# First mixer attention: two heads' scores issued alternately, value outputs in the transposes' banks

## What is computed

```python
def chunked_relpos_attention(h, w_in, q_gain, k_gain, rel_bias, w_out):
    q, k, v = jnp.split(h @ w_in, 3, axis=-1)
    q = rms_norm(q.reshape(B, S, A_HEADS, A_HEAD_DIM), q_gain) * (A_HEAD_DIM ** -0.5)
    k = rms_norm(k.reshape(B, S, A_HEADS, A_HEAD_DIM), k_gain)
    ...
        s = jnp.einsum('bihd,bjhd->bhij', qc, kb).astype(jnp.float32) + bias
        s = jnp.where(valid[None, None, None, :], s, -jnp.inf)
        p = jax.nn.softmax(s, axis=-1).astype(vb.dtype)
        return jnp.einsum('bhij,bjhd->bihd', p, vb)
    ...
    return o @ w_out
```

## Time and profile before

| what | value |
|---|---|
| median of 3 runs | 1064.32 us (1062.67 to 1066.03) |
| the profiled execution | 1061.2 us |
| its span in the trace | 1059.5 us |
| PE, DVE, ACT, POOL busy | 1027.4, 766.1, 550.7, 100.5 us |
| mean granted clock of PE | 0.99 |
| the 19 turns on PE | about 80 to 167 us of the span |

### The profile page before, as it was taken

The page is one execution under the profiler, slowest core; times in us unless marked ns, Lnnn a source line. Parts: engine busy times, 40 slices in busy tenths (PEclk is TensorE's granted clock), DMA queues, the critical chain, the costliest instruction groups (busy, mean ns, idle before and its releaser), DMA issues.

```text
span 1059.5 us, 17084 instructions
## 1 busy us (share of the span) xinstructions
PE 1027.4 (97%) x6050; PEld 898.3 (85%) x6050; DVE 766.1 (72%) x1368; ACT 550.7 (52%) x918; POOL 100.5 (9%) x160
## 2 busy tenths in 40 slices
PE   6999999999999999999999999999999999999997
PEld 5888788899999988889999899999988887778875
DVE  5688878987888677787778756555568786586863
ACT  1457666634545456744444445444346676566662
POOL 0031201000000010010010000000003021030210
PEclk9999999999999989999999999999999999999999
DMA  9876656688787648867685455665436640175401
GB/s 366 297 264 219 228 210 219 202 321 294 266 277 269 232 154 292 294 199 262 207 277 203 140 189 161 197 212 193 161 109 225 201 157 21 66 262 185 165 9 41
DMA packets 57198, 218.46 MB, mean 206 GB/s; under 512 B 6421, under 2 KB 11541, under 8 KB 51001
## 3 DMA queue, kind: packets, MB, share of 16 engines
q1 hardware_dynamic: 48368, 169.24, 46.6%
q0 software_dynamic: 6048, 43.52, 11.6%
q10 hardware_dynamic: 2728, 5.00, 1.5%
HBM read 216.67 MB, written 1.06 MB: 205 GB/s over the span
## 4 chain that ended last, share of the span: by engine, by line
PE 90%; DVE 5%; DMA 2%; ACT 2%; issue 1%; POOL 0%; SPq 0%; ACTq 0%; DVEq 0%
PE ps L1743 26%; PE ps L1744 25%; PE ps L1745 25%; PE ps L1847 2%; PE ps L2225 2%; PE ps L1802 1%; PE ps L1812 1%; DVE w_lo L1008 1%; PE ps L2273 1%; PE ps L2115 1%; PE ps L1792 1%; PE ps L1997 1%; DMA arena<-in_adastream 1%; DMA raw<-in_wstream 1%; PE ps L2254 1%
## 5 line engine op out<-in xcount | busy, mean ns | idle before, releaser
L1008 DVE TENSOR_TENSOR w_lo<-raw,w_hi 128x1024 fp32r<-128x1024 f32 (+1 forms) x312 | 356.2, 1182 | 61.7 <-ACT w_hi L554 56.6
L554 ACT ACTIVATE w_hi<-raw 128x1024 fp32r<-128x1024 f32 (+1 forms) x312 | 307.1, 1021 | 133.7 <-DMA raw<-in_wstream 95.6
L1743 PE MATMUL ps<-h_hi,w_hi 128*128 128x256 f32 x704 | 200.9, 285 | 0.3
L1745 PE MATMUL ps<-h_hi,w_lo 128*128 128x256 f32 x704 | 199.2, 283 | 0.0
L1744 PE MATMUL ps<-h_lo,w_hi 128*128 128x256 f32 x704 | 199.2, 283 | 0.0
L1743 PE MATMUL ps<-w_hi,h_hi 128*128 128x512 f32 (+1 forms) x480 | 191.6, 399 | 7.7 <-DVE h_lo L1087 3.0
L1744 PE MATMUL ps<-w_lo,h_hi 128*128 128x512 f32 (+1 forms) x480 | 185.4, 386 | 0.0
L1745 PE MATMUL ps<-w_hi,h_lo 128*128 128x512 f32 (+1 forms) x480 | 185.3, 386 | 0.0
L1743 PE MATMUL ps<-w_hi,a_hi 128*128 128x512 f32 x352 | 137.3, 390 | 0.7 <-DVE a_lo L1461 0.7
L1743 PEld LDWEIGHTS ps<-h_hi,w_hi 128*128 128x128 f32 x704 | 135.0, 192 | 3.4 <-DVE h_lo L1087 1.3
L1744 PE MATMUL ps<-w_lo,a_hi 128*128 128x512 f32 x352 | 137.2, 390 | 0.0
(11 more groups left out here) (221 smaller groups left out, 1330.6 us busy)
## 6 DMA issues: line engine op xcount, KB each, us to landing
raw<-in_wstream SPq DMA_DIRECT2D x296, 512.0 KB, 5.2
ada_raw<-in_adastream POOLq DMA_DIRECT2D x40, 1024.0 KB, 5.2
ada_raw<-in_adastream SPq DMA_DIRECT2D x4, 1024.0 KB, 9.2
arena<-in_adastream SPq DMA_DIRECT2D x4, 1024.0 KB, 10.8
row<-in_gate_rows ACTq DMA_DIRECT2D x5, 512.0 KB, 4.9
raw<-in_wsmall SPq DMA_DIRECT2D x16, 128.0 KB, 2.2
row<-in_params POOLq DMA_DIRECT2D x2, 769.0 KB, 5.5
x<-in_x SPq DMA_DIRECT2D x1, 1024.0 KB, 9.2
```

The source lines that it names most:

```text
L554: act.activation(w_hi[:, c % SPLIT, at], raw[:, n, 0:width // 2], ACT.Copy)\
L1008: nc.vector.tensor_tensor(w_lo[:, c % SPLIT, at], raw[:, (2 * c + h) % RAW, 0:width // 2], w_hi[:, c % SPLIT, at].bitcast(F32), ALU.subtract)\
L1743: nc.tensor.matmul(dst, sh, mh, start=start, stop=False)
L1745: return nc.tensor.matmul(dst, sl, mh, start=False, stop=stop)
```

## The change

Scores are issued in even turns only, for heads h and h + 1 together: `score_pair(h)` alternates between head h in partitions 0 to 63, into bank 4, and head h + 1 in partitions 64 to 127, into bank 5. Value products go to columns 384 to 511 of bank 6 or 7, beside the transposes, and these now wait for the normalisation (`s_norm`) instead of ACT's copy. Units 2, 3, 6 and 7 go through banks 2, 3, 0 and 1, which are banks of the projection; the waits of turns 6 to 8 change with that. Output groups go to banks 2, 5, 5 and 4. The first group's steps move later: on PE to the end of turn 9, on ACT and DVE from turn 7 to turn 9.

```diff
-HEAD_BANK = (4, 5, 4, 5, 4, 5, 5, 5, 5, 4, 5, 4, 4, 5, 4, 5, 5, 4, 5)
-UNIT_BANK = {0: 4, 1: 5, 4: 6, 5: 7, 2: 4, 3: 4, 6: 5, 7: 4}
+UNIT_BANK = {0: 4, 1: 5, 4: 6, 5: 7, 2: 2, 3: 3, 6: 0, 7: 1}
-OUT_BANK = (4, 5, 4, 4)
+OUT_BANK = (2, 5, 5, 4)
...
@@ ACT, turn h
                 if h == 7:
                     hankel(act, 12, gate[:]).then_inc(s_late[1], 16)
                     hi_part(13, 1, CW)
-                    out_hi(0)
...
                 if h in (8, 9):
                     hi_part(15, h - 8, CW)
+                if h == 9:
+                    out_hi(0)
...
@@ DVE, turn h
                     lo_part(13, 1, CW)
-                    out_lo(0)
...
                 if h in (9, 10):
                     lo_part(15, h - 9, CW)
+                if h == 9:
+                    out_lo(0)
...
@@ PE
-            def bank_read(h):
...
+            def score_pair(h):
+
+                pe.wait_ge(s_qklo, (3, 4, 7, 8)[h // 4])
+                if h >= 2:
+                    pe.wait_ge(s_max, h)
+                if h == 12:
+                    pe.wait_ge(s_h, 6)
+                for qt, (out_at, n) in enumerate(((0, P), (P, S))):
+                    first, second = ps[:, 4, out_at:out_at + n], ps[:, 5, out_at:out_at + n]
+                    (ah, al), (akh, akl) = head_parts(h, qt * P, qt * P + P, 0, n)
+                    (bh, bl), (bkh, bkl) = head_parts(h + 1, qt * P, qt * P + P, 0, n)
+                    nc.tensor.matmul(first, ah, akh, start=True, stop=False)
+                    nc.tensor.matmul(second, bh, bkh, start=True, stop=False)
+                    nc.tensor.matmul(first, ah, akl, start=False, stop=False)
+                    nc.tensor.matmul(second, bh, bkl, start=False, stop=False)
+                    one = nc.tensor.matmul(first, al, akh, start=False, stop=True)
+                    two = nc.tensor.matmul(second, bl, bkh, start=False, stop=True)
+                one.then_inc(s_s, 1)
+                two.then_inc(s_s, 1)
...
                 if h == 6:
                     qkv_step(4, 1, 0)
-                    pe.wait_ge(s_norm, 2)
                     transpose_qk(2)
+                    transpose_qk(3)
                     qkv_step(4, 1, 1)
                 if h == 7:
-                    pe.wait_ge(s_tok, 6)
+                    pe.wait_ge(s_qklo, UNIT_AT[2] + 1)
                     qkv_step(5, 0, 0)
-                    pe.wait_ge(s_qklo, UNIT_AT[2] + 1)
-                    transpose_qk(3)
+                    pe.wait_ge(s_qklo, UNIT_AT[3] + 1)
                     qkv_step(5, 0, 1)
                 if h == 8:
-                    pe.wait_ge(s_qklo, UNIT_AT[3] + 1)
-                    transpose_out(0)
                     qkv_step(5, 1, 0)
-                    pe.wait_ge(s_norm, 5)
                     transpose_qk(6)
+                    transpose_qk(7)
                     qkv_step(5, 1, 1)
-                    pe.wait_ge(s_h, 5)
-                    transpose_qk(7)
...
+                if h < HEADS and h % 2 == 0:
+                    score_pair(h)
+                if h in (11, 15):
+                    pe.wait_ge(s_norm, h - 3)
+                    pe.wait_ge(s_max, h + 1)
+                    transpose_out(h // 4 - 1)
                 if 2 <= h <= HEADS + 1:
                     j = h - 2
                     pe.wait_ge(s_exp, j + 1)
                     if j >= 2:
-                        pe.wait_ge(s_pTc, j - 1)
+                        pe.wait_ge(s_norm, j - 1)
...
+                if h == 9:
+                    pe.wait_ge(s_v, 4)
+                    transpose_out(0)
```

More of the change, by code:

```diff
@@ L1238, in normalise @@
                     o_tok[j // 4][:, :, at:at + DH],
-                    ps[:, HEAD_BANK[j + 3], 384:512].rearrange("p (t d) -> p t d", d=DH),
+                    ps[:, 6 + j % 2, 384:512].rearrange("p (t d) -> p t d", d=DH),
                     recip[:, j, :].unsqueeze(2).to_broadcast([P, TT, DH]), ALU.mult)\
@@ L1310, in _ @@
                         last = nc.vector.tensor_tensor_reduce(
-                            wide[:, h % 3, a:a + n], ps[:, HEAD_BANK[h], a:a + n],
+                            wide[:, h % 3, a:a + n], ps[:, 4 + h % 2, a:a + n],
                             place[:, at:at + n], -1.0, 3e38, ALU.add, ALU.min,
@@ L1975, in _ @@
                     out_step(0, (h - 10) // 2, h % 2)
-                if h == 12:
-                    pe.wait_ge(s_norm, 8)
-                    transpose_out(1)
                 if 14 <= h <= 17:
                     out_step(1, (h - 14) // 2, h % 2)
-                if h == 16:
-                    pe.wait_ge(s_norm, 12)
-                    transpose_out(2)
                 if h == 18:
                     out_step(2, 0, 0)
-                bank_read(h)
                 if h >= 3:
@@ L1997, in _ @@
                             last = nc.tensor.matmul(
-                                ps[:, HEAD_BANK[h], at:at + DH],
+                                ps[:, 6 + j % 2, at:at + DH],
                                 wideT[:, j % 2, (qt + kb) * P:(qt + kb + 1) * P],
```

## The result

The changed kernel takes 1074.22 us (median of 15 runs, 1071.68 to 1081.01); the kernel before, in 15 runs beside it, 1064.32 us. The ratio is 1.0109, with a 95% interval of 1.0090 to 1.0128: 9.9 us by the medians, 11.6 by the ratio, 9.6 to 13.6 by its interval. The profiled execution took 1074.33 us. The forecast was 1073.5, within 1068 to 1077, and slower.

What follows compares the result with a forecast made beforehand. PE was taken to lead at 97% busy, DVE and ACT close behind. With pairing's saving inside the terms, +2.3 - 1.4 + 5.7 + 1.0 + 1.6 = +9.2 us on 1064.3 gave 1073.5 us, range 1068 to 1077.

Steps and rivals of the forecast that it cites:

- Pairs: Attention scores on PE: a pair costs one head's time, so sixteen heads as eight pairs save 7.8 us of PE.
- rival without overlap: Score pairs: the two halves don't run together, a pair takes some 1.6 us, total +11 to +12.5 us (1076); chance 5%.
- Turn 7: PE's second half of chunk 10 waits 4.5 us for unit 3; resumes 2.3 us later, heads 8 and 9 end 0.9 later.
- Turn 10: PE's first output step waits some 8 us for the first output group; maximum 10 goes from 0.9 to 6.6 us later.
- first slow spell: Reduced PE clock behind the stall of turn 7, adding 1.6 us to the sum.
- Turn 12: The pair of heads 12 and 13 waits for the second output group in bank 5, adding 1.0 us.
- The clock: A slow spell behind each stall: the first adds 1.6 us, the second is already in turn 10's delay.
- half case: Both stalls occur, but DVE and ACT make part up and no slow spell follows: +4.7 us (1069); chance 20%.
- other sign: PE bounds the whole stage and operands are ready in time, so all 7.8 us are kept (1056.5); chance 4%.
- from there on I find no cover and no gain: After turn 12, DVE's sums, POOL's loads and ACT's scalings hang on each other, so the delay stays.

Runs made afterwards that it cites:

- e3: Changed kernel with unit 3 back in bank 4 in turn 7 and the first output group back in turns 7 and 8; ratio 0.9985 to the kernel before.
- e4: e3 with each pair's matmuls issued head by head within a query tile instead of alternately; ratio 1.0006 to the kernel before.
- e5: Kernel before, without pairs, with unit 3 moved to bank 3 and chunk 10's second half waiting for it; ratio 1.0053.
- e1: Changed kernel with only the first output group moved back early, through bank 4; unit 3 stays in bank 3; ratio 1.0059 to the kernel before.
- e2: Changed kernel with only unit 3 moved back to bank 4 in turn 7; first output group stays late; ratio 1.0047 to the kernel before.
- e6: Kernel before, without pairs, with the first output group through bank 2 and its steps moved late to turn 9; ratio 1.0073.
- e9: Changed kernel with 34 unread matmuls keeping PE busy ahead of turn 10's wait; ratio 1.0095 to the kernel before.
- e10: Changed kernel with POOL's loads of modulation chunks 13 and 14 issued ahead of its reciprocal roots; ratio 1.0105 to the kernel before.
- e12: e11 with DVE's sums of modulation chunks 13 and 15 a turn later, behind maxima 9 and 13; ratio 0.9943 to the kernel before.
- e8: Kernel before with only POOL's loads of modulation chunks 13 and 14 moved ahead of its reciprocal roots; ratio 1.0009.
- e7: e3 with POOL's loads of modulation chunks 13 and 14 moved ahead of its reciprocal roots; ratio 0.9971 to the kernel before.
- e11: e7 with exponentials transposed before the output group in turns 11 and 15; ratio 0.9992 to the kernel before.

## Why the prediction was right

**Pairs.** Forecast: a pair costs a head's time. Measured: 1.24 us between projection matmuls against 1.21. In the stage PE is busy for 6.3 us less in e3 than before, of the 7.8 worked out; records missing from a trace and slow spells blur that number. The rival without overlap is out.

**Turn 7.** Forecast: PE arrives at 115.9, `unit_lo(3)` ends at 120.35, stall 4.5 us. Measured: its last matmul before starts at 115.40, `unit_lo(3)` at 120.55 and ends at 121.3, stall 5.6 us. PE's extra wait for the head norm, put at 0.7 us, was 0.9 (1.8 against 0.9). POOL's issue came when forecast (105.51; 105.9), but ACT had the chunk 7.6 us later instead of 6.3. In e4 and e5 it was as long (7.7 and 7.6), in e1, e2, e3, e6 and e9 6.1 to 6.3, so this 1.3 us need not be in every execution of the changed kernel. As a part alone, this wait costs 5.6 us (e5).

**Turn 10.** Forecast: maximum 9 held by the sum of chunk 13, output group ready at 142.7, with the first slow spell at 144.3, stall of some 8 us. Measured: maximum 9 at 142.23 with no idle time ahead, `out_lo(0)` from 145.34 to 146.0, stall 8.0 us. Alone it costs 7.8 us (e6).

**Turn 12.** Forecast +1.0 us; from maximum 10 to maximum 12 it is 8.9 us after and 7.65 before, +1.2.

**Sizes.** In the traced execution the stage grew by 13.9 us and not by 9.2. By place: up to maximum 9 it was +4.2 us where 2.5 were forecast (0.9 and 1.6 of clock), from there to maximum 10 +6.8 (5.7), to maximum 12 +1.2 (1.0), and to PV(15) +1.4 (nothing). Two terms were too small. The slow spells lost 2.7 and 2.0 us; 1.6 and 0.9 stood in the sum. And two transfers took longer: 1.3 us at chunk 13, and 1.3 at chunk 18, which ACT had 6.3 us after POOL's issue (171.68 to 177.96) instead of 5.0 (159.28 to 164.26 before). The third slow spell, from 167 to 171 us, cost the path little: from maximum 12 to 13 it is 5.8 us against 5.6.

That a forecast of 1073.5 us comes within 1 us of the median of 1074.22 is partly luck. The profiled execution was forecast at 1070.4 us and took 1074.33, 3.9 more. What made this good is the step from it to the median, for which 3.1 us were added: the kernel before was traced 3.1 us under its median, the changed kernel at its median. Against the interval of 9.6 to 13.6 us the sum of +9.2 was slightly low. The place and kind of each loss were right, their sizes somewhat low.

**The clock.** A slow spell did lie behind each stall. In turn 7 all five traces with the stall have it (changed, e1, e5, e9, e10), and of the nine without only e4, behind a wait of 1.9 us. In turns 9 and 10 every trace but e9's and e12's has half clock, with the stall or without: the kernel before lost 1.7 us there, e3 1.7 and e1 3.4. So how much of the 2.0 us behind the second stall is new isn't shown, and nor is that this stall brought them.

**The half case and the other sign.** ACT and DVE didn't make the stalls up: from maximum 12 on the shift grew. PE's saving alone, the other sign's mechanism, is worth little even without both stalls (1.6 us in e3, not clear of nothing), since DVE's order around the sums of chunks 13 and 15 holds the stage; with that order changed too the kernel is 6 us faster than before (e12). That "from there on I find no cover and no gain" was right for the kernel as changed. How much of e12's gain the kernel before would have by the same reordering, without pairs, wasn't tried, so the pairs' own worth there isn't shown; by POOL's order alone it has no gain that can be told (e8).

## What to carry to other kernels

When a tile moves to another bank, ask which instruction writes that bank next and how far the tile's readers are queued from there: each of the two moved tiles here cost 5 to 8 us, while the pairs were sound and, as e3 shows, needed neither move. A saving on a 97% busy engine is kept only up to the next engine's order; e3 gave 6 us of PE back as idle time until two sums were moved behind maxima (e12). And before choosing between versions 0.3% apart, look at the intervals: e3, e7 and e11 can't be ranked, e12 can be told from e3 and e11 and only just from e7. A gain of two edits together wants the run with each alone, and the one for the sums is missing here.

## What the runs showed of the hardware

- Score matmuls of two heads in different halves of the rows overlap in either order of issue. In e4 matmuls issued a1 a2 a3 b1 b2 b3 start as a1 with b1 at 78.77, then a2 with b2 at 78.93. More than three matmuls of one head before the other's weren't tried. A sentence of the Trainium skill ("TensorE: Matmul & The Clock Gate", Part 3) has matmuls in program order in start and end; for different row halves this trace disagrees on the starts.
- The half clock doesn't need a long stall, and a wait doesn't always bring it. In the kernel before it came from 133 us on the earlier trace rows behind a wait of 0.67 us, and a wait of 1.5 left it at 1.00. The same wait of 1.8 us in turn 11 was followed by 0.50 for 151 to 153 us in e9 and by 1.00 in the changed kernel, where one of 1.8 us in turn 14 was followed by 0.57 for 167 to 171. In e6 the half clock began ahead of the stall.
- The attention begins at one of two times in the traces, 82.4 to 83.0 us (before, changed, e3, e8, e11, e12) or 78.6 to 80.3 (the others). The earlier ones have the lower clock between 20 and 40 us, here the changed kernel and then e7. What makes the difference stays open; it is as large as the effects studied, and a reason to compare within the stage.

```profile
20.00:40.00 20.00, 20.00 (x89) 18.33 (x88) 13.33 (x33) 2.43 (x3) 1.33 (x2) 1.00 1.03 403
```

```profile
20.00:40.00 20.00, 20.00 (x93) 17.45 (x94) 15.68 (x38) 5.58 (x10) 1.33 (x2) 0.55 1.03 403
```
